# Two more weight slots for the gate blocks of every second expert pair, and loops over pairs of pairs

## The chip, the cores and the metric

The kernel runs on one core of a Trainium2 chip. The metric is the device time of one execution in microseconds (us). Three executions of the kernel before took 893.96, 894.42 and 897.92 us; the median is 894.42 us. One further execution was profiled, and every duration and clock time below is from that one.

## The reference

The program is one step of a two-layer model over 256 tokens (128 context, 128 latent) of width 1024, all in fp32. What matters here is its second half in each layer, the mixture of experts: a router picks for each token two of 16 experts, and every expert is a gated pair of matrices. Cut to that:

```python
def _moe(h, w_router, b_router, w_gate, w_up, w_down):
    xt = h.reshape(B * S, D)                          # 256 x 1024
    scores = softmax(xt @ w_router)
    ...                                               # best group, best two experts in it
    gates = ...                                       # 256 x 16, two entries a row are not zero
    hid = silu(einsum('nd,edf->nef', xt, w_gate)) * einsum('nd,edf->nef', xt, w_up)
    hid = hid * gates[..., None]
    y = einsum('nef,efd->nd', hid, w_down)
```

`w_gate` and `w_up` are 1024 x 512 for each expert, `w_down` is 512 x 1024: three blocks of 2 MB. The first half of a layer (called the mixer here) is modulation from a conditioning vector, one input projection, attention, a matrix-memory scan with a final state that is written out, and an output projection with residual.

## The kernel before

**Weights.** All weights stream from HBM through `ring`, six slots of 16 KB in each of 128 partitions, so one slot holds one block of 2 MB. `weight_plan` (L198) gives every load its slot in turn and remembers which load used the slot before. SyncE issues the loads in program order on one queue; before each it waits until TensorE has read what the slot held (`was_read`, L442, and `expert_read`, L432, which waits for the full-bank signal that TensorE's last matmul on that block gives). A load's landing is counted in `slot_landed`. Since the queue works in order, a load that waits holds back all that stand behind it.

**Experts.** TensorE computes two experts at a time: 8 pairs in each of the two layers. A pair `p` has six blocks in this order: two of the gate matrix (slots for `i` = 0, 1), two of up (2, 3), two of down (4, 5). `pair_loads` (L489) loads the six for pair `p`, each waiting for the same block of pair `p - 1`; a loop runs it for pairs 1 to 7. On TensorE, `pair` (L993) does in order: `gate_up` (L934, line L930 holds the matmuls; first the gate blocks into bank 1, then the up blocks into bank 2), `scatter` of the pair before (L967), the first half of `gather` for the next pair (L918), `turn_hidden` (L948), the second half of `gather`, and `down` (L958). Pair 0 and pair 7 are written out, pairs 1 to 6 are one loop with a body of one pair. ScalarE and VectorE have loops of their own beside it (exponential, reciprocal, products, copies out of PSUM) and signal back through `bank_read`.

**Around the experts.** Ahead of the expert loads, SyncE issues the mixer's: six projection blocks, eight modulation blocks, two of the output projection (L484) and, in the first layer alone, four modulation blocks of the next layer (L486). The mixer's scan ends with `joined(3)` on VectorE (L1561), which takes bank `("num", 1, 3)`. In the same stretch GpSimd issues on a queue of its own the write of the final state, 512 KB (L1811), and 4 KB of its second part (L1813); GpSimd, ScalarE (L1252) and VectorE (L1595) wait for both to land (`state_out`) before they use memory again, VectorE just ahead of `sdot` (L1598), `awr` (L1603) and the first residual after the output projection (L1394), which TensorE needs at L582.

**Memory.** The mixer's tiles (L281 to L295) and the experts' tiles (L309 to L328) lie over each other, both from the same start. `sq2` holds squares and scaled activations up to the modulation that writes `hT`; `gpick` is the gate-weighted selection that GpSimd builds (L1818) and `scat` its transpose, read by `scatter`; `awr` and `lr` are used by the router, before `ye` has its first use.

## Time and profile before

| | |
|---|---|
| profiled execution, time | 898.56 us |
| profiled execution, span from first to last instruction | 896.3 us |
| median of three executions | 894.42 us |
| mean granted TensorE clock | 0.977 |
| TensorE matmul busy | 842.0 us, 94% of the span |
| VectorE, ScalarE, GpSimd busy | 30%, 20%, 5% |
| moved by DMA | 289.31 MB, mean 323 GB/s |
| experts, layer 0 and layer 1 | about 224 to 460 us and 649 to 885 us |

The profile's clock starts at the first instruction of the span. PE is TensorE's matmul side, PEld its weight loads, DVE VectorE, ACT ScalarE, POOL GpSimd, SP SyncE; a q behind the name is that engine's instruction queue. "SPq L496 DMA_DIRECT2D ... x2" is the issue of two transfers, not their flight; a landing is counted from the issue to the semaphore.

### The profile page before, as it was taken

How to read it: one execution, taken by the hardware profiler on the slowest of the kernel's cores; microseconds unless marked ns; L12 is line 12 of the kernel's file. 1: busy time of each engine (PE TensorE's matmuls, PEld its weight loads, DVE VectorE, ACT ScalarE, POOL GpSimd, SP SyncE). 2: the span in 40 equal slices, each digit the busy share in tenths (PEclk: the TensorE clock that was granted, in tenths of full speed). 3: DMA queues.
4: the chain of work that ended last, by engine and by line, in shares of the span. 5: the costliest groups of instructions: out<-in, count | busy, mean ns of one | idle time of the engine just before them, and what ended most of it. 6: DMA issues, size and time to landing. Idle time of an engine off the chain costs nothing.

```text
span 896.3 us, 10655 instructions
## 1 busy us (share of the span) xinstructions
PE 842.0 (94%) x4330; PEld 471.6 (53%) x4332; DVE 270.3 (30%) x503; ACT 179.5 (20%) x354; POOL 46.3 (5%) x50
## 2 busy tenths in 40 slices
PE   3799999998999999999979999999699999999996
PEld 2255646684545543555345555668554554355533
DVE  0203185525311222022231317552531122202222
ACT  3203124506111100111031212450511110011101
POOL 4000040100100000000000004000010000000000
PEclk9799999999999999999999999999789999999999
DMA  8993459758799999999995254975239999999991
GB/s 300 401 388 115 182 208 405 290 188 331 288 401 424 429 426 429 429 428 430 419 383 197 94 188 179 410 285 188 94 149 399 424 430 428 431 427 428 429 389 48
DMA packets 39682, 289.31 MB, mean 323 GB/s; under 512 B 3288, under 2 KB 5520, under 8 KB 21216
## 3 DMA queue, kind: packets, MB, share of 16 engines
q1 hardware_dynamic: 38000, 285.77, 78.4%
q0 software_dynamic: 1408, 2.97, 1.1%
q8 instruction: 26, 0.43, 0.2%
q10 hardware_dynamic: 240, 0.08, 0.0%
q14 instruction: 8, 0.07, 0.0%
HBM read 286.44 MB, written 2.37 MB: 322 GB/s over the span
## 4 chain that ended last, share of the span: by engine, by line
PE 84%; DMA 6%; DVE 4%; ACT 4%; issue 1%; SPq 0%; ACTq 0%; DVEq 0%
PE ps L930 24%; PE ps L620 14%; PE ps L958 12%; PE ps L918 7%; PE ps L850 6%; PE ps L967 6%; DMA ring<-in_w_mod 3%; PE ps L632 3%; PE ps L545 3%; DMA ring<-in_w_e_up 2%; DVE xT L1394 1%; ACT xe L1286 1%; PE ps L672 1%; PE ps L770 1%; ACT hT L1115 1%
## 5 line engine op out<-in xcount | busy, mean ns | idle before, releaser
L930 PE MATMUL ps<-ring,xe 128*64 128x512 f32 x1024 | 223.0, 593 | 0.4 <-DMA ring<-in_w_e_up 0.2
L930 PEld LDWEIGHTS ps<-ring,xe 128*64 128x64 f32 x1024 | 74.6, 137 | 144.9 <-issue 144.7
L620 PE MATMUL ps<-ring,hT 128*128 128x512 f32 (+1 forms) x320 | 130.2, 568 | 4.5 <-ACT hT L1115 4.5
L958 PE MATMUL ps<-ring,hidT 128*64 128x512 f32 x512 | 113.4, 595 | 1.6 <-ACT hidT L1298 1.6
L620 PEld LDWEIGHTS ps<-ring,hT 128*128 128x128 f32 x320 | 62.2, 196 | 69.4 <-issue 65.9
L1712 DVE COPY ye<-ps 128x512 f32<-128x512 f32 x16 | 11.1, 691 | 214.9 <-PE ps L958 214.9
L918 PE MATMUL ps<-pick,htok 128*128 (+1 forms) x512 | 67.9, 290 | 7.4 <-ACT xe L1286 3.5
L958 PEld LDWEIGHTS ps<-ring,hidT 128*64 128x64 f32 x512 | 36.3, 137 | 67.4 <-issue 65.9
L918 PEld LDWEIGHTS ps<-pick,htok 128*128 128x128 f32 x512 | 64.7, 203 | 11.9 <-ACT xe L1286 6.8
L967 PE MATMUL ps<-scat,ye 128*128 (+1 forms) x256 | 59.5, 386 | 1.8 <-DVE ye L1712 1.8
L850 PE MATMUL ps<-hT,ring 128*128 128x256 f32 x256 | 58.3, 387 | 0.0
L967 PEld LDWEIGHTS ps<-scat,ye 128*128 128x128 f32 x256 | 47.4, 190 | 20.5 <-issue 14.8
L1286 ACT ACTIVATE xe<-ps 128x512 f32<-128x512 f32 x32 | 19.1, 597 | 179.2 <-PE ps L918 179.2
L1697 DVE RECIPROCAL ex<-ex 128x512 f32<-128x512 f32 x16 | 53.6, 3353 | 0.6
L850 PEld LDWEIGHTS ps<-hT,ring 128*128 128x128 f32 x256 | 49.1, 195 | 7.3 <-issue 0.8
L545 PE MATMUL ps<-ring,cT 128*32 128x512 f32 x384 | 47.0, 616 | 5.9 <-DMA ring<-in_w_mod 4.2
L1695 DVE TENSOR_SCALAR ex<-ex 128x512 f32<-128x512 f32 x16 | 6.8, 427 | 120.4 <-ACT ex L1291 120.4
L1291 ACT ACTIVATE ex<-ps 128x512 f32<-128x512 f32 x16 | 9.6, 597 | 148.7 <-PE ps L930 148.7
L632 PE MATMUL ps<-hT,ring 128*128 128x256 f32 x128 | 28.7, 383 | 0.0
L1394 DVE SCALAR_TENSOR_TENSOR xT<-ps,modc,xT 128x128 f32<-128x128 f32 x64 | 17.4, 342 | 33.0 <-PE ps L850 30.4
L632 PEld LDWEIGHTS ps<-hT,ring 128*128 128x128 f32 x128 | 24.0, 190 | 4.7 <-issue 1.6
L1790 POOL TENSOR_TENSOR qkr<-qk 128x640 f32<-128x640 f32 x4 | 5.0, 1251 | 407.3 <-DVE vx L1465 407.3
(257 smaller groups left out, 650.6 us busy)
## 6 DMA issues: line engine op xcount, KB each, us to landing
ring<-in_w_e_gate SPq DMA_DIRECT2D x32, 2048.0 KB, 13.4
ring<-in_w_e_up SPq DMA_DIRECT2D x32, 2048.0 KB, 16.7
ring<-in_w_e_down SPq DMA_DIRECT2D x32, 2048.0 KB, 12.2
ring<-in_w_mod SPq DMA_DIRECT2D x24, 2048.0 KB, 8.5
ring<-in_w_in SPq DMA_DIRECT2D x10, 2048.0 KB, 21.1
ring<-in_w_out SPq DMA_DIRECT2D x4, 2048.0 KB, 15.4
ring<-in_w_in SPq DMA_DIRECT2D x2, 1024.0 KB, 17.7
C<-in_state_C POOLq DMA_DIRECT2D x2, 512.0 KB, 9.2
```

What stands on the lines that cost most here:

```text
L545: mm = pe.matmul(ps[7][32 * g:32 * g + 32, :], cT[:, c:c + 32], w[:, k, g * WB:(g + 1) * WB], start=(c == 0), stop=(c == NB * (KD - 1)))
L620: mm = pe.matmul(bank[:, 0:width], hT[:, k, b * P:(b + 1) * P], w[:, k, :], start=(k == 0), stop=(k == KD - 1))
L632: mm = pe.matmul(bank[:, j * TOK:(j + 1) * TOK], w[:, k, h * MD:(h + 1) * MD], hT[:, k, :], start=(k == 0), stop=(k == KD - 1))
L850: mm = pe.matmul(bank[:, j * TOK:(j + 1) * TOK], w[:, k, c:c + P], cat[:, k, :], start=(k == 0), stop=(k == KD - 1))
L918: mm = pe.matmul(bank[:, k * P:(k + 1) * P], htok[:, b, 4 * half + k, :], pick[:, b, bass.ds(2 * p, 2), :].rearrange("p e c -> p (e c)"), ...
L930: mm = pe.matmul(ps[1 + u][64 * j:64 * j + 64, :], xe[:, k, j * SLOTS:(j + 1) * SLOTS], w[j][:, k, :], start=(k == 0), stop=(k == KD - 1))
L958: mm = pe.matmul(ps[3 - half][64 * j:64 * j + 64, :], hidT[:, k, j * SLOTS:(j + 1) * SLOTS], w[j][:, k, half * 512:(half + 1) * 512], star ...
L967: mm = pe.matmul(ps[4 + dj // 2][:, (dj % 2) * TOK:(dj % 2 + 1) * TOK], ye[:, dj * P:(dj + 1) * P], scat[:, bass.ds(p, 1), :].rearrange("p ...
L1286: act.activation(xe[:, 4 * half:4 * half + 4, :], bank[:, :].rearrange("p (k c) -> p k c", k=4), ACT.Copy).then_inc(read, 1)
L1394: ins = dve.scalar_tensor_tensor(x, bank[:, c:c + P], modc[:, l % 2, gate * KD + 2 * i + j, b:b + 1], x, ALU.mult, ALU.add)
L1697: dve.reciprocal(ex[:, :], ex[:, :]).then_inc(silu_step, 1)
L1712: dve.tensor_copy(ye[:, 512:1024], ps[2][:, :]).then_inc(bank_read[2], 1)
```

## The change

Two tiles of 16 KB a partition, `extra`, are laid behind the experts' tiles. They take the gate blocks of pairs 1, 3, 5 and 7; the gate blocks of pairs 0, 2, 4 and 6 stay in the ring slots `i` = 0 and 1, which are now used 4 times a layer and not 8. The room comes from tiles that now share memory: `gpick` and `sq2` are one tile (`lists`), `scat` lies in `hT`, `awr` and `lr` in `ye`. GpSimd waits for all modulation steps before it writes `gpick`, since they read `sq2`.

On SyncE the blocks of a layer are now issued in this order: gate of pair 1 into `extra` (after a wait for `("num", 1, 3)` to be taken), all six of pair 0, up and down of pair 1; then three times, for q = 1 to 3: gate of pair 2q (waits for the gate of pair 2q - 2), up and down of pair 2q, gate of pair 2q + 1 into `extra` (waits for the gate of pair 2q - 1), up and down of pair 2q + 1. The next layer's loads into slots 0 and 1 wait for the gate of pair 6.

On TensorE pairs 1 to 6 are a loop of three passes with a body of two pairs, the first of which reads its gate blocks from `extra`. The loops of ScalarE and VectorE are as before.

```diff
--- before.py
+++ after.py
@@ -199,12 +199,15 @@
 
     n = 0
     last = [None] * RING
+    uses = [0] * RING
     plan = {}
 
-    def put(key):
+    def put(key, times=1):
         nonlocal n
-        plan[key] = (n % RING, n // RING, last[n % RING])
-        last[n % RING] = key
+        slot = n % RING
+        plan[key] = (slot, uses[slot], last[slot])
+        last[slot] = key
+        uses[slot] += times
         n += 1
 
     for i in range(SEC_SLOTS):
@@ -221,8 +224,7 @@
             for i in range(SEC_SLOTS):
                 put(("mod", *sec, i))
         for i in range(RING):
-            put(("expert", l, i))
-        n += RING * (PAIRS - 1)
+            put(("expert", l, i), PAIRS // 2 if i < 2 else PAIRS)
     return plan
 
 
@@ -306,19 +308,15 @@
 
 
         with ExitStack() as experts:
-            sq2 = sb("sq2", [P, KD, TOK], where=experts)
+            lists = sb("lists", [P, KD * TOK], where=experts)
             htok = sb("htok", [P, NB, KD, P], where=experts)
             pick = sb("pick", [P, NB, E, SLOTS], where=experts)
-            gpick = sb("gpick", [P, NB, E, SLOTS], where=experts)
-            scat = sb("scat", [P, PAIRS, TOK], where=experts)
             xe = sb("xe", [P, KD, P], where=experts)
             ex = sb("ex", [P, F], where=experts)
             hid = sb("hid", [P, KF, P], where=experts)
             hidT = sb("hidT", [P, KF, P], where=experts)
             ye = sb("ye", [P, D], where=experts)
             rt = sb("rt", [P, 16, 32], where=experts)
-            awr = sb("awr", [P, (KD * NB + 1) * E], where=experts)
-            lr = sb("lr", [P, TOK], where=experts)
             cmpa = sb("cmpa", [P, 8, 4, 4], where=experts)
             cmpb = sb("cmpb", [P, 8, 4, 4], where=experts)
             spick = sb("spick", [P, NB, SLOTS], where=experts)
@@ -326,6 +324,12 @@
             sscat = sb("sscat", [SLOTS, TOK], where=experts)
             sex = sb("sex", [P, KF, SLOTS], where=experts)
             shid = sb("shid", [P, KF, SLOTS], where=experts)
+            extra = sb("extra", [P, 2, KD * WB], where=experts)
+        sq2 = lists[:, :].rearrange("p (k t) -> p k t", k=KD)
+        gpick = lists[:, :].rearrange("p (b e c) -> p b e c", b=NB, e=E)
+        scat = hT
+        awr = ye[:, 0:(KD * NB + 1) * E]
+        lr = ye[:, D - TOK:D]
         xtok = ring[:, 5, 0:NB * D].rearrange("p (b d) -> p b d", b=NB)
         otok = sq2[:, :, :].rearrange("p k t -> p (k t)").rearrange("p (b d) -> p b d", b=NB)
         rowsin = prob[0:ROWS_L, 0:DEPTH * P].rearrange("p (l c) -> p l c", l=DEPTH)
@@ -336,6 +340,7 @@
         bank_full = [sem(f"bank_full{i}") for i in range(8)]
         bank_read = [sem(f"bank_read{i}") for i in range(8)]
         slot_landed = [sem(f"slot_landed{i}") for i in range(RING)]
+        extra_landed = [sem(f"extra_landed{j}") for j in range(2)]
         mod_read = sem("mod_read")
         dve_step, act_step = sem("dve_step"), sem("act_step")
         const_in, x_in, cond_in, rows_in, small_in = (sem(n) for n in (
@@ -450,7 +455,7 @@
                 elif key[0] == "out":
                     full(sp, (("mix", 2 * key[2] + 1), key[1]))
                 elif key[0] == "expert":
-                    expert_read(key[1], key[2], PAIRS - 1)
+                    expert_read(key[1], key[2], PAIRS - 2 if key[2] < 2 else PAIRS - 1)
                 else:
                     full(sp, ((key[0], 1), key[1]))
 
@@ -486,19 +491,40 @@
                     load_section(*sec)
                 blocks = ((w_gate, 0, KD), (w_gate, 1, KD), (w_up, 0, KD), (w_up, 1, KD), (w_down, 0, KF), (w_down, 1, KF))
 
-                def pair_loads(p):
-                    for i, (w, j, k) in enumerate(blocks):
-                        slot, _, last = weights["expert", l, i]
-                        if isinstance(p, int):
-                            was_read(last)
+                def block(i, p, dst, landed):
+
+                    w, j, k = blocks[i]
+                    sp.dma_start(dst.rearrange("p (k n) -> p k n", k=k), w[l, 2 * p + j]).then_inc(landed, 16)
+
+                def ring_block(i, p, before=None):
+
+                    slot, _, last = weights["expert", l, i]
+                    if before is None:
+                        was_read(last)
+                    else:
+                        expert_read(l, i, before)
+                    block(i, p, ring[:, slot, :], slot_landed[slot])
+
+                def extra_blocks(p, before=None):
+
+                    for j in range(2):
+                        if before is None:
+                            taken(sp, (("num", 1, MH - 1), l))
                         else:
-                            expert_read(l, i, p - 1)
-                        sp.dma_start(ring[:, slot, :].rearrange("p (k n) -> p k n", k=k),
-                                     w[l, 2 * p + j]).then_inc(slot_landed[slot], 16)
-
-                pair_loads(0)
-                with sp.Fori(1, PAIRS) as p:
-                    pair_loads(p)
+                            expert_read(l, j, before)
+                        block(j, p, extra[:, j, :], extra_landed[j])
+
+                extra_blocks(1)
+                for i in range(RING):
+                    ring_block(i, 0)
+                for i in range(2, RING):
+                    ring_block(i, 1, 0)
+                with sp.Fori(1, PAIRS // 2) as q:
+                    for i in range(RING):
+                        ring_block(i, 2 * q, 2 * q - 2 if i < 2 else 2 * q - 1)
+                    extra_blocks(2 * q + 1, 2 * q - 1)
+                    for i in range(2, RING):
+                        ring_block(i, 2 * q + 1, 2 * q)
                 with sp.If(largest(sp, l) > SLOTS):
                     for i in SPILL_BLOCKS:
                         expert_read(l, i, PAIRS - 1)
@@ -528,9 +554,9 @@
             def done(key, ins):
                 ins.then_inc(bank_full[banks[key][0]], 1)
 
-            def landed(key, p=0):
+            def landed(key):
                 slot, n, _ = weights[key]
-                pe.wait_ge(slot_landed[slot], p * 16 + 16 * (n + 1))
+                pe.wait_ge(slot_landed[slot], 16 * (n + 1))
                 return ring[:, slot, :]
 
             def section_rows(l, s, *which):
@@ -920,9 +946,21 @@
                                            start=(b == 0), stop=(b == NB - 1))
                     mm.then_inc(bank_full[0 if bank is ps[0] else 3], 1)
 
-                def into_hidden(p, u):
-
-                    w = [landed(("expert", l, 2 * u + j), p).rearrange("p (k n) -> p k n", k=KD) for j in range(2)]
+                def expert_block(i, p, q, odd):
+
+                    slot, n, _ = weights["expert", l, i]
+                    if i >= 2:
+                        pe.wait_ge(slot_landed[slot], p * 16 + 16 * (n + 1))
+                    elif odd:
+                        pe.wait_ge(extra_landed[i], q * 16 + 16 * (PAIRS // 2 * l + 1))
+                        return extra[:, i, :]
+                    else:
+                        pe.wait_ge(slot_landed[slot], q * 16 + 16 * (n + 1))
+                    return ring[:, slot, :]
+
+                def into_hidden(p, u, q, odd):
+
+                    w = [expert_block(2 * u + j, p, q, odd).rearrange("p (k n) -> p k n", k=KD) for j in range(2)]
                     for k in range(KD):
                         if isinstance(p, int) and p == 0 and k % 4 == 0:
                             taken(pe, (("first", k // 4), l))
@@ -931,14 +969,14 @@
                                            w[j][:, k, :], start=(k == 0), stop=(k == KD - 1))
                     mm.then_inc(bank_full[1 + u], 1)
 
-                def gate_up(p):
+                def gate_up(p, q, odd):
 
                     if not (isinstance(p, int) and p == 0):
                         pe.wait_ge(bank_read[0], 2 * p + base[0])
                     pe.wait_ge(bank_read[1], p + base[1])
-                    into_hidden(p, 0)
+                    into_hidden(p, 0, q, odd)
                     pe.wait_ge(bank_read[2], 2 * p + base[2])
-                    into_hidden(p, 1)
+                    into_hidden(p, 1, q, odd)
 
                 def turn_hidden(p):
 
@@ -948,9 +986,9 @@
                         mm = pe.transpose(ps[3][:, k * P:(k + 1) * P], hid[:, k, :], ident)
                     mm.then_inc(bank_full[3], 1)
 
-                def down(p):
-
-                    w = [landed(("expert", l, 4 + j), p).rearrange("p (k n) -> p k n", k=KF) for j in range(2)]
+                def down(p, q, odd):
+
+                    w = [expert_block(4 + j, p, q, odd).rearrange("p (k n) -> p k n", k=KF) for j in range(2)]
                     pe.wait_ge(bank_read[3], 2 * p + (base[3] + 1))
                     for half in range(2):
                         for k in range(KF):
@@ -990,8 +1028,8 @@
                         pe.matmul(ps[4 + i][:, :], zeros[:, :], zeros[:, 0:1].broadcast_to([P, 512]), start=True, stop=False,
                                   skip_group_check=True)
 
-                def pair(p, first=False, last=False):
-                    gate_up(p)
+                def pair(p, q, odd, first=False, last=False):
+                    gate_up(p, q, odd)
                     if first:
                         scatter_maps()
                     else:
@@ -1003,16 +1041,17 @@
                         gather(p + 1, 1)
                     if first:
                         clear_sums()
-                    down(p)
+                    down(p, q, odd)
 
                 pe.wait_ge(pick_ready, 2 * l + 1)
                 taken(pe, *[(("tok", i), l) for i in range(4)])
                 gather(0, 0)
                 gather(0, 1)
-                pair(0, first=True)
-                with pe.Fori(1, PAIRS - 1) as p:
-                    pair(p)
-                pair(PAIRS - 1, last=True)
+                pair(0, 0, False, first=True)
+                with pe.Fori(1, PAIRS // 2) as q:
+                    pair(2 * q - 1, q - 1, True)
+                    pair(2 * q, q, False)
+                pair(PAIRS - 1, PAIRS // 2 - 1, True, last=True)
                 scatter(PAIRS - 1, last=True)
 
                 def spill(e, c):
@@ -1814,6 +1853,7 @@
                 pool.wait_ge(state_out, 16 * STATE_OUTS * (l + 1))
                 pool.wait_ge(gates_ready, l + 1)
                 pool.wait_ge(pick_ready, 2 * l + 2)
+                pool.wait_ge(h_a, HA_STEPS * (l + 1))
                 for b in range(NB):
                     ins = pool.tensor_tensor(gpick[:, b, :, :], pick[:, b, :, :],
                                              per_col(rt[:, R_G, b * E:(b + 1) * E], SLOTS), ALU.mult)
```

## Rows read from the trace of the kernel before

**Rows 1.** Page: busy us of an engine, share of the span, instructions

```profile
PE 842.0 (94%) x4330; PEld 471.6 (53%) x4332; DVE 270.3 (30%) x503; ACT 179.5 (20%) x354; POOL 46.3 (5%) x50
```

**Rows 2.** TensorE's waits, whole span: waited for, us in total, times, longest

```profile
PE ps L918 <- ACT xe L1286: 3.5, 14, 0.3
...
PE ps L930 <- DMA ring<-in_w_e_up: 0.2, 1, 0.2
```

**Rows 3.** Busy us (PE, PEld, DVE, ACT, POOL), PEclk, DMA share, GB/s

```profile
403.00:431.70 28.70, 28.45 (x150) 14.29 (x148) 5.97 (x5) 2.88 (x5) 0.00 (x0) 1.00 1.00 428
```

**Rows 4.** Chain of waits, two successive pairs of layer 0: start, us, what

```profile
287.01 13.73 PE ps L930 x64
...
315.94 13.73 PE ps L930 x64
```

**Rows 5.** Chain of waits, pair 7 of layer 0

```profile
416.94 21.69 DMA ring<-in_w_e_up
```

**Rows 6.** Chain of waits, pair 7 of layer 1

```profile
864.16 0.13 issue
```

**Rows 7.** SyncE's timeline: first issue, us to the last, transfers

```profile
148.42 34.89 SPq L470 DMA_DIRECT2D ring<-in_w_mod  x4
...
237.12 0.88 SPq L496 DMA_DIRECT2D ring<-in_w_e_gate  x2
243.82 0.81 SPq L496 DMA_DIRECT2D ring<-in_w_e_up  x2
258.13 0.81 SPq L496 DMA_DIRECT2D ring<-in_w_e_down  x2
265.15 0.86 SPq L496 DMA_DIRECT2D ring<-in_w_e_gate  x2
271.86 0.81 SPq L496 DMA_DIRECT2D ring<-in_w_e_up  x2
287.05 0.81 SPq L496 DMA_DIRECT2D ring<-in_w_e_down  x2
...
438.58 29.03 SPq L470 DMA_DIRECT2D ring<-in_w_in  x6
...
575.72 15.11 SPq L496 DMA_DIRECT2D ring<-in_w_e_gate  x2
```

**Rows 8.** DMA issues at 237.12, 244.2, 258.13: size, us to landing

```profile
ring<-in_w_e_gate SPq DMA_DIRECT2D x1, 2048.0 KB, 7.7
...
ring<-in_w_e_up SPq DMA_DIRECT2D x1, 2048.0 KB, 16.8
...
ring<-in_w_e_down SPq DMA_DIRECT2D x1, 2048.0 KB, 8.0
```

**Rows 9.** Chain of waits, layer 1: joined(3)

```profile
592.66 0.44 DVE work L1561
```

**Rows 10.** Page, DMA queues: packets, MB, share of 16 engines

```profile
q8 instruction: 26, 0.43, 0.2%
```

**Rows 11.** DMA queues, 258 to 287 us

```profile
q8 instruction: 1, 0.02, 0.2%
```

**Rows 12.** DMA queues, 287 to 432 us (the only queue with packets)

```profile
q1 hardware_dynamic: 4259, 62.00, 100.6%
```

**Rows 13.** DMA issues, 590 to 612 us: size, us to landing

```profile
out_new_state_C<-qk POOLq DMA_DIRECT2D x1, 512.0 KB, 9.1
out_new_state_n<-nst POOLq DMA_DIRECT2D x1, 4.0 KB, 4.7
```

**Rows 14.** GpSimd's timeline, layer 1: start, us of the issue

```profile
595.17 0.93 POOL L1811 DMA_DIRECT2D out_new_state_C<-qk  x1 [41.96 <-ACT qk L1238]
601.18 0.51 POOL L1813 DMA_DIRECT2D out_new_state_n<-nst  x1 [5.08 <-DVE nst L1586]
```

**Rows 15.** VectorE's timeline, layer 1, first residual

```profile
609.30 0.16 DVE L1598 COPY sdot<-ps 2x16 f32<-2x16 f32 x1
...
609.98 1.12 DVE L1394 SCALAR_TENSOR_TENSOR xT<-ps,modc,xT 128x128 f32<-128x128 f32 x4
```

**Rows 16.** Chain of waits, layer 1, first use of that residual

```profile
615.73 0.57 PE ps L582 x8
```

## The prediction

> **What bounds the kernel now.** I first read the busy times on the page: TensorE's matmul side is busy for 94% of the span [rows 1]. An average over stages says little, so next come TensorE's own waits. In all of the experts the reader should see only two kinds: 14 short waits for `xe` (3.5 us together, 0.3 at most) and a single wait of 0.2 us for a weight block, an up block [rows 2]. Third, the busy table of one expert pair: TensorE is busy for 28.45 of 28.70 us at full clock while the DMA engines are at 100%, moving 428 GB/s [rows 3]. So both run flat out, and the question is which of them sets the end. The chain of waits answers it: two successive pairs begin their gate matmuls at 287.01 and 315.94, a period of 28.93 us in which no transfer stands [rows 4]. Only in pair 7 of layer 0 does the chain go through a transfer, the second up block: issue at 416.94, 21.69 us, so it lands at 438.63 [rows 5]. In layer 1 the same place costs a gap of 0.13 us [rows 6]. TensorE sets the pace; the stream is just not late until the last pair.
>
> **Why the stream gets late, and when it starts.** SyncE's timeline [rows 7] gives the issues: gate of pair 1 at 237.12, up at 243.82, down at 258.13, gate of pair 2 at 265.15, up at 271.86, down at 287.05. The first down block of pair 1 lands 8.0 us after its issue [rows 8], at 266.1. From it to the second up block of pair 7 are 35 further blocks (six for each of pairs 2 to 7, less the one counted), which land by 438.6: 172.5 / 35 = 4.93 us a block, 29.6 us a pair, against TensorE's 28.93. The stream loses about 0.6 us a pair and has used up its lead by pair 7.
>
> **The extra blocks.** The issue is 4 MB earlier in each layer, worth 2 x 4.93 = 9.9 us of transfer. Where does this lead go? The order on the one queue after pair 1's up is the same before and after: down 1, gate 2, up 2, down 2, gate 3, and so on. Down 1 waits for TensorE to read down 0, at 258.13, in both. With gate 1 already landed, up 1 (issue still 243.82) would go out at once: a block into an idle stream lands after 7.7 us [rows 8], the second 4.9 later, at about 256.4 and not at 244.2 + 16.8 = 261.0. Then the engines stand idle until down 1 comes at 258.13. From there on the stream was never idle before (its next blocks were always issued before the last had landed), so the blocks take the same 4.93 us each in the same order. Gate 2 is requested at 258.95, right behind down 1, and not at 265.15, but it queues behind down 1 in either case. The 9.9 us of lead are lost in the wait for the down slot. What is left is that down 1 meets an idle queue: 7.7 us to landing and not 8.0, so that everything behind it, up to pair 7's up block, is some 0.3 us earlier. That is just enough for the 0.2 us wait in layer 0 and the 0.13 us gap in layer 1. Bounds: nothing gained, or both gone: 0 to -0.35 us. I take -0.3, because the first block's 0.3 is read directly.
>
> **The loads behind the experts.** The next layer's first two projection blocks no longer wait for pair 7's gate matmuls; they are issued behind down 7, at about 432.5 and not 438.58 [rows 7]. They queue behind up 7 and down 7 anyway, and TensorE does not use them until 469.6, when the activations are ready. 0 us, bounded by 0 on both sides as no wait for a block stands there in the chain.
>
> **Pair 0 and the place of the wait.** In layer 0 the extra blocks go out after the last modulation block, at 148.42 + 34.89 = 183.3 [rows 7]; joined(3) was long done. They end about 10 us later, while pair 0's blocks are needed from 229.9. In layer 1 no modulation blocks stand between, and gate 0 was issued at 575.72 [rows 7]. Now the wait for joined(3), at 592.66 + 0.44 = 593.1 [rows 9], stands ahead of it. Gate 0, gate 1 and up 0 are queued behind it. Gate 0 moves 18 us later; five blocks released at once need 5 x 4.93 = 25 us, so they have landed by about 620, up 1 and the two down blocks (issued at 609 to 631) by 640. First use is at 655.5: That is 15 us of cover, so 0 us.
>
> **Loops, waits and shared tiles.** GpSimd's new wait is for activations that TensorE's transposes have read before the selection exists: 0 us. ScalarE's and VectorE's loops are unchanged. On TensorE each block has one wait as before, with a register value. Only one start in a pair is exposed to the sequencer, the second gather half behind `xe`, with 0.25 us (3.5 / 14) [rows 2]. If its address sums took up to 0.1 us more or less (an estimate: less than half of that wait), 12 passes would give -1.2 to +1.2 us. I take 0. A loop's back edge costs nothing that shows: the period across it is the 28.93 us of [rows 4].
>
> **Sum.** 898.56 - 0.3 = 898.3 us for the profiled execution, whose span is 896.3. It lies 4.1 us above the median of 894.42 of the runs shown; from the median, 894.42 - 0.3 = 894.1 us.
>
> **Rival 1, slower: TensorE has to fetch its loop body again.** The body grows from one pair, some 300 records (x150 and x148 in [rows 3]) and 40 waits and register steps, to two. Instruction packets have a queue of their own: 26 of them, 0.43 MB, 16 KB each [rows 10]. One arrives while TensorE runs the loop's first pass, 258 to 287 us [rows 11], and none from 287 to 432, five more passes [rows 12]: so this body is held at no cost, and what was fetched last beside it. If a body of twice the size is not held, each of the four back edges (two a layer) stalls until a packet has come. Price: a small transfer under load took 4.7 us [rows 13], so 4 x 4.7 = 19 us, 913 us; if every packet of the body were missed (three or four a pass, 12 to 16 in all), 55 to 75 us, up to 970. It decides from the point where the body is larger than what TensorE holds. For it: no row shows a body of that size held. Against it: a body of more than one packet, with one more fetched during the first pass, already runs without a fetch.
> [...]
>
> **Rival 2, a little slower: the state's write is crowded out in layer 1.** The final state's 512 KB are issued at 595.17 and its second part at 601.18 [rows 14]; they land after 9.1 and 4.7 us [rows 13], by 605.9. The extra blocks now start at 593.1 and fill the engines to 618. VectorE waits for both landings ahead of `sdot` at 609.30 and the residual at 609.98 [rows 15], which TensorE first needs at 615.73 [rows 16]; residual and what precedes it take 1.8 us, so a landing up to 613.9 costs nothing. If the big write took twice as long (18.2 us, 613.4) and the small one 4.7 us behind it, 618.1, TensorE would stand 4.2 us: 898.3 us. Against it: most of the write already ran beside ring blocks.
>
> **Rival 3, faster by more.** If the stream in layer 0 and 1 had been held back by more than the traced execution shows (the unprofiled ones have no rows), a lead kept in full would save at most what is late; to win 0.5% each layer must be 2.2 us late at pair 7, and the argument on down 1 would have to fail. 889 us.
>
> **How the numbers follow.** Two medians of this kernel can't be told from no change within 0.5%, 4.5 us. Chances: forecast 0.78, rival 1 0.10, rival 2 0.07 (nearly all of it still within 0.5%), rival 3 0.05. So faster 0.05, same 0.84, slower 0.11. Range: the forecast's own bounds are 894.42 - 0.35 - 1.2 = 892.9 and 895.6; executions here spread over 893.96 to 897.92, and rival 2 reaches 898.3. I give 892 to 898.8; rival 1 stays outside.
>
> **What would show it.** In the profile after: the period of two pairs is 57.9 us; down 1 lands 7.7 us after an issue at about 258; no wait for an up block in pair 7; `extra` issued at about 183 and 593; the state's write landing before 613. TensorE stalls at every second pair beginning with instruction packets in the looping stretch would be rival 1; a wait at L582 for the residual rival 2; a first down block much before 258 would mean that my order argument is wrong.

## The result and the profile after

The changed kernel takes **899.79 us** (median of 20 executions, 894.26 to 902.02); the kernel before, executed beside it on the same chip, takes 896.34 us (20 executions, 893.23 to 898.70). The ratio is **1.0030, with a 95% interval of 1.0016 to 1.0043** (here and below the ratio is not exactly the quotient of the two medians, which is 1.0038 here). So the change costs about 3 us where 0.3 us of gain was forecast: it lies outside the predicted range, and on the other side of no change. Part of the distance to the forecast is its starting point: it set out from 894.42 us, the median of three executions, and with twenty the kernel before is at 896.34. So of the 5.7 us between 894.1 and 899.79 the start has 1.9 and the change 3.8 (0.3 forecast as a gain and 3.45 lost). The profiled execution took 899.7 us with a span of 897.5 us (before: 898.56 and 896.3 us). These two differ by 1.1 us only: the changed kernel's trace is 3.1 us ahead when the last scatter of layer 0's experts starts (455.56 against 458.68), and 2.6 us of that stand already at the first gather of the experts (221.82 against 224.46). The medians carry the sign and the traces carry the place.

The page, busy us of each engine, answers to [rows 1]. VectorE, ScalarE and GpSimd are unchanged to 0.1 us, and TensorE is 1.9 us *less* busy, yet the kernel is slower. A loss with less busy time points to idle time, and the thing to look for is a new gap on the engine that sets the pace.

```profile
PE 840.1 (94%) x4332; PEld 469.3 (52%) x4332; DVE 270.3 (30%) x503; ACT 179.6 (20%) x354; POOL 46.3 (5%) x50
```

What the prediction said of the loop holds. Chain of waits, two successive second pairs of layer 0 with one pair between them (start, us, what), which answers to [rows 4]: from 284.37 to 342.22 are 57.85 us, twice the 28.93 us of before, and no step stands at the border of the two-pair body.

```profile
284.37 13.73 PE ps L968 x64
...
313.30 13.73 PE ps L968 x64
...
342.22 13.73 PE ps L968 x64
```

SyncE's timeline (first issue, us to the last, transfers) answers to [rows 7]. The first `extra` block is issued at 180.69 and the second use at 285.50; gate 2 moved from 265.15 to 256.68. But down 1 is issued at 255.49, which is 14.3 us behind its up block as before ([rows 7]: 243.82 to 258.13): it waits for the release of its own slot, and the lead that the two new slots gave in gate blocks is lost to that wait, once a pair.

```profile
180.69 0.94 SPq L497 DMA_DIRECT2D extra<-in_w_e_gate  x2
...
241.18 0.80 SPq L497 DMA_DIRECT2D ring<-in_w_e_up  x2
255.49 0.80 SPq L497 DMA_DIRECT2D ring<-in_w_e_down  x2
256.68 0.95 SPq L497 DMA_DIRECT2D ring<-in_w_e_gate  x2
269.22 0.81 SPq L497 DMA_DIRECT2D ring<-in_w_e_up  x2
284.41 0.81 SPq L497 DMA_DIRECT2D ring<-in_w_e_down  x2
285.50 0.86 SPq L497 DMA_DIRECT2D extra<-in_w_e_gate  x2
```

DMA issues at 255.49 (size, us to landing), against the 8.0 us of [rows 8]: down 1 lands after 7.7 us, the figure of an idle start, as forecast.

```profile
ring<-in_w_e_down SPq DMA_DIRECT2D x1, 2048.0 KB, 7.7
```

TensorE's waits over the whole span (waited for, us, times, longest) answer to [rows 2]. The waits inside the pairs are the old ones. The first line is what grew: the wait of the norm sums for their squares, which before stood there once, with 1.5 us, and is now there twice, with 4.3 us.

```profile
PE ps L593 <- ACT work L1141: 4.3, 2, 2.7
PE ps L944 <- ACT xe L1325: 3.5, 14, 0.3
...
PE ps L968 <- DMA ring<-in_w_e_up: 0.2, 1, 0.2
```

**The new gap.** TensorE's timeline between the last scatter of layer 0's experts and the first projection of layer 1 (start, us, line, tiles, count, and in brackets the idle time before it and what is thought to have ended it). The kernel before:

```profile
458.68 3.69 PE L967 MATMUL ps<-scat,ye 128*128 128x256 f32 x16 [0.88 <-DVE ye L1712]
462.21 3.98 PE L567 MATMUL ps<-work,ones 128*128 128x256 f32 x16
469.62 5.80 PE L620 MATMUL ps<-ring,hT 128*128 128x512 f32 x9 [3.43 <-ACT hT L1115]
```

and the changed kernel (the scatter matrix now shares its memory with `hT` and goes by that name):

```profile
455.56 3.69 PE L1005 MATMUL ps<-hT,ye 128*128 128x256 f32 x16 [0.88 <-DVE ye L1751]
461.99 3.69 PE L593 MATMUL ps<-work,ones 128*128 128x256 f32 x16 [2.74 <-ACT work L1141]
469.11 6.36 PE L646 MATMUL ps<-ring,hT 128*128 128x512 f32 x8 [3.43 <-ACT hT L1154]
```

From the start of the last scatter to the start of the norm sums it was 3.53 us and is 6.43 us: **2.9 us more, with TensorE idle**. The trace names ScalarE's squares as what ended the wait. ScalarE's timeline (same columns) says otherwise. After:

```profile
457.92 0.63 ACT L1141 ACTIVATE work<-xT 128x512 f32<-128x512 f32 x1 [6.04 <-DVE xT L1433]
458.89 0.63 ACT L1141 ACTIVATE work<-xT 128x512 f32<-128x512 f32 x1 [0.34 <-DVE xT L1433]
459.92 0.63 ACT L1141 ACTIVATE work<-xT 128x512 f32<-128x512 f32 x1 [0.40 <-DVE xT L1433]
460.96 0.63 ACT L1141 ACTIVATE work<-xT 128x512 f32<-128x512 f32 x1 [0.40 <-DVE xT L1433]
...
465.71 0.47 ACT L1148 ACTIVATE rstd<-ps,eps 128x256 f32<-128x256 f32 x1 [2.62 <-PE ps L593]
```

The first square is done at 458.55, and the sums need the squares one by one: in the kernel before they began at 462.21, 1.2 us behind the start of the first square at 461.04. Here they begin 4.1 us behind it. ScalarE then waits 2.62 us for TensorE, where it had not waited before. So TensorE itself is late, and the releaser in the bracket is merely the last semaphore event before the start. The queue of instruction packets gives a hint of what TensorE stood for. DMA queues of the changed kernel, windows 458 to 460 and 463 to 466 us (packets, MB, share of the 16 engines in that window); in 440 to 458 and 460 to 463 us this queue has no packet:

```profile
q8 instruction: 1, 0.02, 3.5%
...
q8 instruction: 1, 0.02, 2.3%
```

In the kernel before there is one packet in 440 to 456 us and one in 460 to 463 us, and TensorE runs on between scatter and sums. What lies between scatter and sums in the code is the test for an overfull expert, `with pe.If(count > SLOTS)`, whose body holds the whole code for such experts and is never run with this input. TensorE has to jump over it. The body has 96 fp32 matmuls and 2 transposes; in the trace such a matmul is two weight loads and two matmuls (L930: 32 calls in the source, 64 matmul records, and as many weight loads as matmuls in [rows 1], 4332 and 4330), so with its waits and loop steps it is some 410 instructions, an estimate. The reading, which the experiments test: in the kernel before, the code behind the jump had come with the packet ahead of it; in the changed kernel that packet starts only when the jump has been made, and the engine stands until it is there. The packet falls in 459.0 to 459.5 us, and TensorE goes on at 461.99.

**The clock behind it.** Busy time of each engine in 466 to 476 us (us; PE, PEld, DVE, ACT, POOL busy, then granted clock, DMA share, GB/s): kernel before, then after.

```profile
466.00:476.00 10.00, 6.57 (x12) 2.89 (x12) 4.68 (x12) 5.78 (x13) 0.00 (x0) 0.83 1.05 371
```

```profile
466.00:476.00 10.00, 6.89 (x10) 3.03 (x11) 4.68 (x12) 5.29 (x11) 0.00 (x0) 0.66 0.84 298
```

The granted clock is 0.50 in 470.3 to 473.7 us of the kernel before and in 467.7 to 474.5 us of the changed one: a mean of 0.83 over these 10 us is 3.4 us at half, 0.66 is 6.8 us. Just before the projection TensorE is idle for 3.43 us in both kernels; the changed one has its 2.7 us ahead of the norm sums besides. The stretch doesn't follow the kernel strictly, as the experiments show, so this part of the loss is counted with care below.

The DMA issues from 590 to 612 us (KB, us to landing), against [rows 13], with the first residual on VectorE:

```profile
out_new_state_C<-qk POOLq DMA_DIRECT2D x1, 512.0 KB, 11.8
out_new_state_n<-nst POOLq DMA_DIRECT2D x1, 4.0 KB, 7.2
```

```profile
611.31 0.16 DVE L1637 COPY sdot<-ps 2x16 f32<-2x16 f32 x1
```

The state's write takes 2.7 us longer beside the extra blocks (issued at 595.68 and 601.68, landed by 608.9), and `sdot` starts at 611.31, so nothing waits for it: rival 2's contention is real, and of the 3.4 us of slack before (605.9 to 609.30) 2.4 us are left.

### The profile page after: what moved, and what is told of

It reads as the page before. It is cut to its first block, busy times and chain, and to the rows that moved or that the text cites. A ratio compares the mean times of both kernels' runs of the same rounds, so it can differ in the third digit from the quotient of the medians.

```text
span 897.5 us, 10618 instructions
## 1 busy us (share of the span) xinstructions
PE 840.1 (94%) x4332; PEld 469.3 (52%) x4332; DVE 270.3 (30%) x503; ACT 179.6 (20%) x354; POOL 46.3 (5%) x50
## 4 chain that ended last, share of the span: by engine, by line
PE 85%; DMA 6%; DVE 4%; ACT 4%; issue 1%; SPq 1%; ACTq 0%; DVEq 0%
PE ps L968 24%; PE ps L646 14%; PE ps L996 12%; PE ps L944 7%; PE ps L876 6%; PE ps L1005 6%; DMA ring<-in_w_mod 3%; PE ps L658 3%; PE ps L571 3%; DMA ring<-in_w_e_up 2%; DVE xT L1433 1%; ACT xe L1325 1%; PE ps L698 1%; PE ps L796 1%; ACT hT L1154 1%
## 5 line engine op out<-in xcount | busy, mean ns | idle before, releaser
L968 PE MATMUL ps<-ring,xe 128*64 128x512 f32 x768 | 167.7, 592 | 0.2 <-DMA ring<-in_w_e_up 0.2
L968 PEld LDWEIGHTS ps<-ring,xe 128*64 128x64 f32 x768 | 55.8, 137 | 108.5 <-issue 108.2
L1005 PE MATMUL ps<-hT,ye 128*128 (+1 forms) x256 | 59.5, 385 | 1.8 <-DVE ye L1751 1.8
L1005 PEld LDWEIGHTS ps<-hT,ye 128*128 128x128 f32 x256 | 47.3, 190 | 20.6 <-issue 14.8
L968 PE MATMUL ps<-extra,xe 128*64 128x512 f32 x256 | 56.3, 592 | 0.0
L876 PEld LDWEIGHTS ps<-hT,ring 128*128 128x128 f32 x256 | 48.7, 193 | 7.2 <-issue 0.8
L968 PEld LDWEIGHTS ps<-extra,xe 128*64 128x64 f32 x256 | 18.4, 137 | 36.5 <-issue 36.5
```

Of the source, the lines that this page charges most:

```text
L876: mm = pe.matmul(bank[:, j * TOK:(j + 1) * TOK], w[:, k, c:c + P], cat[:, k, :], start=(k == 0), stop=(k == KD - 1))
L968: mm = pe.matmul(ps[1 + u][64 * j:64 * j + 64, :], xe[:, k, j * SLOTS:(j + 1) * SLOTS], w[j][:, k, :], start=(k == 0), stop=(k == KD - 1))
L1005: mm = pe.matmul(ps[4 + dj // 2][:, (dj % 2) * TOK:(dj % 2 + 1) * TOK], ye[:, dj * P:(dj + 1) * P], scat[:, bass.ds(p, 1), :].rearrange("p ...
```

## The experiments

Three batches of four kernels; within a batch the kernels share one chip and its runs of the kernel before (medians 895.88, 896.95 and 896.66 us). The place that each is read at is the same throughout: the time from the start of the last scatter of layer 0's experts to the start of the norm sums, 3.5 us without the stall and 6.4 to 6.6 us with it, called the gap here. Two theories stood at the start: **A**, the code of TensorE moved and it now waits for instructions at the jump over the never-run code; **B**, the extra slots' loads and shared tiles make something late.

**The jump moved by padding.** First try: 100 waits that are always fulfilled, put into TensorE's stream early on, move all later code by 100 instructions.

```diff
+            for _ in range(100):
+                pe.wait_ge(ones_set, 1)
             pe.wait_ge(const_in, 16)
```

On the changed kernel:

> The changed kernel with 100 more instructions on TensorE, waits that are already satisfied, ahead of its first work (where it stands idle for 12 us). They move nothing but the place of TensorE's code against the blocks in which it is fetched. Theory A (the loss is a late instruction block behind layer 0's experts, where TensorE jumps over the code for overfull experts, which never runs): the norm sums there start within 0.5 us of the last scatter's end instead of 2.9 us after it, no instruction packet falls right behind the jump, and the median is 2 to 3 us below the changed kernel's, 896 to 898. Theory B (the loss comes from the extra blocks' transfers or from shared memory): the 2.9 us gap stays and so does the median, 899 to 900.

Measured 899.65 us, ratio 1.0036 [1.0018, 1.0054]; the gap is still there, 6.44 us. Theory A's forecast for this run was wrong, and this run alone would speak for B. The same edit on the kernel before:

> The kernel before with the same 100 satisfied waits on TensorE at the start. Theory A: the shift takes the jump's target out of the blocks already fetched, so the norm sums behind layer 0's experts start 2 to 3 us late and the median rises by 2 to 3 us, to 898.5 to 899.5, with no other change. Theory B: the same as the kernel before within 0.1%.

Measured 903.6 us (4 executions), ratio 1.0093 [1.0064, 1.0123]; the gap appears, 6.57 us. So padding alone, with no other edit, brings the stall to the kernel before, and nothing of the extra slots is needed for it. That the loss is about 8 us (0.93%) rather than 3 isn't explained by this gap.

**The loop alone.** The kernel before, with only TensorE's loop written over two pairs; slots, loads and tiles as before.

```diff
-                with pe.Fori(1, PAIRS - 1) as p:
-                    pair(p)
+                with pe.Fori(1, PAIRS // 2) as q:
+                    pair(2 * q - 1)
+                    pair(2 * q)
```

> The kernel before with TensorE's loop of three passes over two pairs alone; no extra slots, memory and transfers as before. Theory A: TensorE's code ahead of the jump is as long as in the changed kernel (5 instructions less in 3630), so the gap of 2.9 us appears and the median is that of the changed kernel, 899 to 900. Theory B: no loss, 896.

Measured 899.89 us, ratio 1.0038 [1.0019, 1.0057]: the whole loss of the change. TensorE's timeline, gap 6.51 us:

```profile
454.15 3.69 PE L967 MATMUL ps<-scat,ye 128*128 128x256 f32 x16 [0.88 <-DVE ye L1713]
460.66 3.69 PE L567 MATMUL ps<-work,ones 128*128 128x256 f32 x16 [2.81 <-ACT work L1103]
```

Theory B falls here as the cause of the loss: no extra slot, load or shared tile is in this kernel. The changed kernel once more, in the same batch:

> The changed kernel itself, unchanged, beside the others on one chip. Both theories: slower than the kernel before by 0.2 to 0.4%, with the 2.9 us gap in its trace; whether its lower clock shares (0.975 to 0.987) belong to the loss is to be read from the clocks of its rounds against those of the kernel before.

Measured 898.56 us, ratio 1.0028 [1.0010, 1.0046], gap 6.45 us.

**How far does the jump's place matter?** From the first four traces a rule was made: a stall wherever the jump lands more than about 512 instructions behind the last block border that TensorE crossed. A block is taken to be what one packet brings. Its length in instructions, and with it every distance, is the author's estimate: from 44.7 to 281.2 us of the kernel before ten packets come and TensorE has 1231 matmuls and 1232 weight loads, 246 a packet, its waits and register steps not counted. The kernel before, at 511, had no stall, and the nearest with one was at 591; the 512 was chosen between the two. The rule gave 128 pads as a cure for the changed kernel, and no stall for the kernel before with 200 pads.

```diff
-            for _ in range(100):
+            for _ in range(128):
```

> The changed kernel with 128 satisfied waits at TensorE's start. The four traces so far put the loss in one place: the norm sums behind layer 0's experts start 3.1 us late wherever the jump over the overfull-expert code (some 410 instructions) lands more than about 512 instructions behind the last block border that TensorE crossed; by the instruction packets that distance is 511 in the kernel before, 591 in the changed one, 611 with e2's padding, and e1's 100 put a border exactly at the end of the loop (684). Theory A2: with 128 the next border falls inside pair 7, the distance is about 465, the gap goes (scatter to norm sums 3.5 us and not 6.4) and the median falls to 896 to 897. Rival B2: doubling the loop body itself costs the gap, wherever the borders lie: it stays, 899 to 900.

Measured 899.26 us, 1.0016 [0.9998, 1.0034]; the gap stays, 6.45 us.

> The kernel before with 200 satisfied waits at TensorE's start. A2: distance about 455, so no gap, scatter to norm sums 3.5 us, median as the kernel before within 0.15% (so 100 of them cost 3 us and 200 nothing). A rival, that such waits at the start cost time by themselves: slower than with 100, 903 or more.

(The same edit with 200, on the kernel before.) Measured 900.88 us, 1.0040 [1.0017, 1.0062]; gap 6.50 us in the trace. The rule is wrong: where the block borders lie, counted in instructions from the start, doesn't by itself tell a hit (no stall) from a miss (the stall). The next edits change the length of the jump instead.

**The never-run code made shorter.** In the changed kernel, the hidden-layer matmuls of the overfull-expert code are cut, which makes the jump 240 instructions shorter. What is computed for an overfull expert is wrong with it; with this input none is.

```diff
-                        for f in range(KF):
-                            for k in range(KD):
+                        for f in range(1):
+                            for k in (0, KD - 1):
```

> The changed kernel, with 60 of the 64 hidden-layer matmuls of the code for overfull experts left out on TensorE (that code is never taken with these inputs). The jump is 240 instructions shorter, some 350 from the last border. A2: no gap, 896 to 897. B2, or anything that lies in the extra blocks: gap and 899 to 900.

Measured 896.37 us, 0.9992 [0.9975, 1.0009]. The changed kernel's loss is gone, by removing instructions that are never executed. An instruction packet still falls at the jump, in 459.5 to 460.0 us, and nothing waits for it; the second one of the changed kernel, 6 us later, is not there. TensorE's timeline, gap 3.53 us as in the kernel before:

```profile
456.07 3.69 PE L1005 MATMUL ps<-hT,ye 128*128 128x256 f32 x16 [0.88 <-DVE ye L1751]
459.60 3.69 PE L593 MATMUL ps<-work,ones 128*128 128x256 f32 x16
```

**Work for TensorE in the idle stretches.** The kernel before, with matmuls of a tile of zeros into a PSUM bank that is free: 12 behind layer 1's norm sums and 4 times 8 in its router stretch.

```diff
+                if l > 0:
+                    fill(("modcol", l, 0), 12)
```

> The kernel before with matmuls of a zero tile into the idle bank 7 where TensorE waits: 12 behind the norm sums at the start of layer 1, and four times 8 in layer 1's router stretch, where layer 0 has the modulation's work. The traces show TensorE's clock at half for 3.4 to 6.8 us behind layer 0's experts and for 17 us in layer 1's router stretch. If that comes from TensorE standing idle, the clock stays up, the first projection block of layer 1 takes 14 us and not 16 to 17, and the layer-1 gather before pair 0 3.6 us and not 5.8: 3 to 5 us faster than the kernel before, 891 to 893. If the clock falls anyway, the same time or up to 2 us slower, because the filler delays the work behind it.

Measured 894.93 us, 0.9996 [0.9974, 1.0019]: no gain that can be measured. The 3 to 5 us expected did not come. In its profile the granted clock behind the experts is 1.00 over 466 to 476 us, against 0.83, but the router stretch is no shorter: from the first use of the residual to the first gate matmul of pair 0 it takes 40.2 us (610.48 to 650.67), and 39.8 in the kernel before (615.66 to 655.48). So only the first of the two places was worth another try.

**The never-run code made longer.** The kernel before, with 20 more matmuls (80 instructions) in the never-run body and nothing else.

```diff
+                    for k in range(20):
+                        mm = pe.matmul(ps[2][:, 7 * SLOTS:8 * SLOTS], w[:, k % KD, 3:F:KF],
+                                       xe[:, 0, 0:SLOTS], start=False, stop=(k == 19), skip_group_check=True)
```

> The kernel before with 20 more matmuls (80 instructions) in the code for overfull experts, which never runs. Nothing that executes is changed or moved ahead of the jump. The padding of f1 and f2 did not follow the border sums, f3's shorter jump cured the gap. Theory A (a jump too far for what TensorE has fetched ahead): the kernel before was close to the edge, so scatter to norm sums takes 6.4 us and not 3.5, two instruction packets fall at and 6 us behind the jump, and the median is 2 to 3 us up, 898.5 to 900. Rival (what matters is what runs ahead of the jump, not its length): no gap, 896 to 897.

Measured 901.58 us (6 executions), 1.0053 [1.0035, 1.0071]. One pair a turn, the old slots, every executed instruction where it was up to the jump, and the stall is there. TensorE's timeline; the last line is behind the same jump in layer 1, where this kernel alone of the fourteen traced stands a second time, for 0.80 us in the middle of the output transposes, with an instruction packet in 888 to 890 us (this may be part of why the median is up by 4.9 us and not by 3):

```profile
454.92 3.69 PE L967 MATMUL ps<-scat,ye 128*128 128x256 f32 x16 [0.88 <-DVE ye L1715]
461.45 3.69 PE L567 MATMUL ps<-work,ones 128*128 128x256 f32 x16 [2.83 <-ACT work L1105]
...
891.91 1.58 PE L1067 MATMUL ps<-cst,xT 128*128 128x128 f32 x13 [0.80 <-issue]
```

Its instruction packets fall as in the changed kernel: one in 458 to 460 us, right behind the jump, and one in 463 to 466 us.

```profile
q8 instruction: 1, 0.02, 3.4%
...
q8 instruction: 1, 0.02, 2.3%
```

This and the shorter jump are the pair that settles it: they change nothing but the length of what is jumped over, and with it where the jump lands, one in each kernel, and each turns the gap into the other kernel's. No executed instruction, load or tile is different, so a wait for data is out as the cause.

**The jump hinted.** The changed kernel with a branch hint, placed a pair ahead of the jump, and the test written so that the likely way is the taken branch. All code stays and everything is computed. The edit does two things at once, the hint and the turned test; which of them is needed was not run apart.

```diff
+                loc = pe.mark_branch_hint_location("LikelyTaken")
                 pair(PAIRS - 1, last=True)
...
-                with pe.If(count > SLOTS):
+                pe.br_lt(count, SLOTS + 1, on_true=f"fits{l}", on_false=f"spills{l}").branch_hint(loc)
+                with nc.body(f"spills{l}", valid_engines=[mybir.EngineType.PE]):
...
+                    pe.br(f"fits{l}")
+                nc.switch_bb(f"fits{l}")
```

> [...] If the gap were no instruction fetch, nothing changes: 899 to 900.

Theory A forecast a gap of 3.5 us and a median of 896 to 896.5 us. Measured 895.71 us, 0.9985 [0.9966, 1.0004]. The gap is 3.53 us, and the packet that had come in 463 to 466 us is gone from there (the one in 458 to 460 us remains and nothing waits for it). Inside pair 7 there is one packet, in 438 to 441 us, as in the changed kernel, and none in 441 to 458 us in either. So the traces show the stall and the packet behind it gone with the hint, and no packet that comes earlier for it; how the hint does it is not shown.

```profile
455.31 3.69 PE L1005 MATMUL ps<-hT,ye 128*128 128x256 f32 x16 [0.88 <-DVE ye L1755]
458.84 3.69 PE L593 MATMUL ps<-work,ones 128*128 128x256 f32 x16
```

The same hint on the kernel before:

> The kernel before with the same hint. Its target was fetched in time already, so every theory says the same time as before within 0.15%; what the hint itself costs would show here.

Measured 895.86 us, 0.9991 [0.9973, 1.0010]. The two hinted kernels lie within 0.15 us of each other: **the extra slots by themselves gain or lose nothing** that these runs can show, and the prediction's 0.3 us of gain is too small to be told from nothing here. In this kernel's trace the norm sums start on time but stand for 0.33 us after eleven matmuls and go on at 461.55 us, 2.0 to 2.5 us behind the start of a packet (in 459.0 to 459.5 us).

**Hint and zero matmuls together**, on the changed kernel, with the fill behind layer 1's norm sums only:

> g2 with 12 matmuls of a zero tile behind the norm sums at the start of layer 1 (f4's filler, only there). In f4 the clock stayed up there and the first projection blocks took 14.9 us and not 16.6 to 17.7. If that holds: 1 to 2.5 us below g2, 894 to 895, and faster than both kernels.

Measured **892.55 us, 0.9958 [0.9942, 0.9974]**: faster than both kernels, 0.4% below the kernel before. TensorE's timeline, where the 3.4 us of idle time before the first projection (3.6 us with the hint alone) are now 1.0 us, as the zero matmuls fill them:

```profile
457.40 3.68 PE L600 MATMUL ps<-work,ones 128*128 128x256 f32 x16
461.14 2.56 PE L590 MATMUL ps<-zeros 128*128 128x512 bf16 x11
464.70 10.54 PE L655 MATMUL ps<-ring,hT 128*128 128x512 f32 x24 [1.01 <-ACT hT L1167]
```

In its chain of waits the first 32 projection matmuls take 13.97 us, where they took 15.67 us in the kernel before and 16.66 us after the change. One row each, of the kernel with hint and fill, of the kernel with the hint alone, of the kernel before and of the changed kernel:

```profile
464.70 13.97 PE ps L655 x32
```

```profile
466.13 13.97 PE ps L646 x32
```

```profile
469.62 15.67 PE ps L620 x32
```

```profile
469.11 16.66 PE ps L646 x32
```

The second row is the one to stop at: without any fill the trace of the hint alone has the full clock too. From the last scatter to the first projection it takes 10.82 us (455.31 to 466.13), with the fill 10.83 us (453.87 to 464.70). So this pair of traces shows no gain at the place of the fill. Over all traces, both with the fill have a granted clock of 1.00 from 463 to 476 us; of the twelve without it ten have a half-clock stretch there and two have none (the hint alone, and the changed kernel's second profile). A half-clock stretch that comes less often would fit the lower median; it is not shown, and the same fill in the kernel before gave no gain clear of noise.

## Why the prediction was wrong, point by point

**TensorE sets the pace, 28.93 us a pair.** Right: 57.85 us for two pairs, before and after [rows 4].

**The lead of two gate blocks is lost, since down 1 waits for its slot.** Right, and it is the step on which the sum for the slots stood: down 1 keeps its 14.3 us behind up 1, lands after 7.7 us, and the hinted kernels with and without the extra slots take 895.71 and 895.86 us. The gain of 0.3 us did not show even in the traces: the up wait of pair 7, 0.2 us, is gone in layer 0 and stands in layer 1 instead, where the kernel before had none and where the changed kernel's second profile has 0.4 us; the 0.13 us of [rows 6] is still there with 0.14. So the sum's one gain was mis-sized, by an amount far below what a median can show.

**Loads behind the experts.** Right: the next layer's loads are issued at 431.05 where they were issued at 438.58 [rows 7], and the first projection waits for ScalarE's `hT` in both kernels, so nothing is gained by it. Pair 0 is right as well: `extra` goes out at 180.69 and 593.61, and no wait for a block stands at pair 0.

**"Loops, waits and shared tiles", priced at 0 us with a bound of 1.2 us.** This is the step that failed. The loop itself is free, as said: behind the changed kernel's first pass there is no instruction packet from 304 to 432 us, nor from 740 to 876 us in layer 1, and no stall at the border of the body. The sum stopped at the loop. The longer body also changes where all code behind it lies and, as this document reads it, what is already fetched when TensorE comes to the jump. Behind the loop stand pair 7, the last scatter and that jump over some 410 instructions that are never run. It costs nothing in the kernel before and 2.9 us after the change. The row that should have raised the question was on the table: with [rows 10] there are 26 instruction packets, few enough to ask of each one what TensorE does when it comes, and one of them comes beside that jump.

**Rival 1, instruction fetches at the back edges, 913 us.** Its kind of cost was the right one and its place was wrong. It had a chance of 0.10 and a price that was a fetch for every back edge; what came was one stall, at one jump. The changed kernel has 28 instruction packets of 0.46 MB instead of the 26 of [rows 10]. Against the rival the prediction set that the loop of before ran without fetches. That was weak evidence: by the prediction's own estimate of three or four packets for two pairs, one pair is no more than two packets, and one packet came in its first pass (258 to 287 us). The changed kernel's loop is the test: two packets come in the first pass of its body, 255 to 313 us, one more in the 5 us ahead of it, and none from 313 to 439 us, so its back edges cost no fetch. At the forward jump the runs show a stall or none, by the jump's length, though the three paddings show that length is not all. A loop that runs without packets says nothing of a forward jump in the same kernel.

**Rival 2, the state's write.** Did not come: the landing at 608.9 us is 2.4 us before `sdot` starts. **Rival 3** did not come either (its 889 us should read 890: 894.42 less twice 2.2).

**The size.** The loss of the medians is 3.45 us. Of it 2.9 us is the gap, seen in all eight traces of kernels whose jump is late (6.43 to 6.57 us, against 3.52 to 3.53 us in the others). The rest, 0.55 us, is within what the interval leaves open (1.4 to 3.9 us for the whole). The clock has a part that one trace can't size: the first 32 projection matmuls take 2.7 us more than at a granted clock of 1.00 after the change and 1.7 us more before it, which would be 1.0 us, but the changed kernel's second profile (e4 above) has a granted clock of 1.00 over the same stretch, and the shortened kernel, without stall, has 0.68. So half-clock stretches there vary between executions of one kernel. Hint and fill against hint alone are 892.55 and 895.71 us, beside the same runs of the kernel before. That difference is measured; that it comes from the clock in this stretch is argued only, since the trace of the hint alone has the full clock here too.

**What stays open.** Which lengths of jump hit and which miss: the paddings of 100 in the changed kernel, 128 in it and 200 in the kernel before all stalled against a forecast made from block borders. Why the 2.9 us are longer than a packet's own transfer, about 1.1 us (3.5% of 16 engines over 2 us, an estimate): the rings' transfers fill the DMA engines in that stretch (share 1.04 to 1.07 from 458 to 466 us), but a kernel with the same jump and idle DMA engines wasn't run. Why the kernel before with 100 pads lost about 8 us with 3 us more in the gap: only four executions stand behind it, the traced one is the fastest of them (900.3 us), and its trace shows no second gap of that kind. And where the fill's 3 us in the medians come from.

## What to carry to other kernels

Sum a change of loop structure over the code behind the loop too: every forward jump over never-run code in TensorE's stream (a fallback, an overflow case) is a place where the engine may stand for instructions, as it did here for 2.9 to 3.0 us in eight of fourteen traces, and whether it does went by the length and place of code, with no change in the work. Read it in the trace as a gap that has a releaser long past, with an instruction packet that starts at the gap (a packet alone is no sign: the cured kernels have one at the jump too, in 459.5 to 460.0 us with the shorter jump and in 458 to 460 us with the hint); what cured it here was a branch hint a pair ahead with the likely way as the taken branch, or a shorter fallback. And when a change comes out some tenths of a per cent off with all its own steps confirmed, run it once with only the code moved before looking for a story in its data flow.

## What the runs showed of the hardware

- TensorE stood for 2.9 to 3.0 us at a forward jump while the rings were loading, in eight of fourteen traces; the instruction packets are of 16 KB (28 with 0.46 MB in the changed kernel), and one starts at the jump (459.0 to 459.5 us in the changed kernel, where TensorE goes on at 461.99). That it is this packet that TensorE waits for is the reading that fits all runs. Making the jumped-over code 80 instructions longer turned a hit into a miss (gap 3.53 to 6.53 us), 240 shorter turned a miss into a hit (6.43 to 3.53 us).
- A loop body of two pairs ran without an instruction packet for 128 us in layer 0 (304 to 432 us) and 136 us in layer 1 (740 to 876 us). A hint a pair ahead of the jump, with the test turned, removed the stall (gap 3.53 us for 6.43).
- Behind layer 0's experts the granted clock over 466 to 476 us differs between executions of one kernel: 0.66 and 1.00 in the changed kernel's two traces. The 32 projection matmuls there take 13.97 us at a granted clock of 1.00 and 16.66 us where 6.8 us of the stretch are at 0.50. Both traces with twelve matmuls of zeros in the idle time ahead have 1.00, and so has one of the hint alone. In the router stretch 32 more such matmuls made it no shorter (40.2 us for 39.8).
- The state's 512 KB took 11.6 to 11.8 us to land in the seven traces with the extra slots, where two more blocks of 2 MB are queued ahead of it, and 9.1 to 9.2 us in the seven without.
